# Where three small products stand in a feed-forward stage, and one more behind each layer norm's first sums

## The chip, the cores and the metric

The kernel runs on one core of one Trainium2 chip. The metric is the device time of one execution in microseconds (us); less is better. The kernel before took 3452.98 us in the median of three runs (3448.43 to 3456.45 us).

## The reference

Two blocks follow each other, each with two layers, on 256 tokens of width 2048. The first is an attention block, the second alternates mixers with feed-forward stages; the change lies in the second:

```
for layer in range(DEPTH):                                   # DEPTH = 2
    x = layer_norm(ALPHA * x + mixers[layer](x), *ln1[layer])
    x = layer_norm(ALPHA * x + conv_ffn(x, *ffns[layer]), *ln2[layer])

def layer_norm(x, g, b, eps=LN_EPS):                         # over the 2048 features of a token
    mu = xf.mean(-1, keepdims=True)
    var = jnp.square(xf - mu).mean(-1, keepdims=True)
    return ((xf - mu) * lax.rsqrt(var + eps) * g + b).astype(x.dtype)

def conv_ffn(x, w_gate, w_val, conv_w, conv_b, w_down):      # 2048 -> 5632 -> 2048
    h = causal_dwconv(x @ w_gate, conv_w) + conv_b
    return (jax.nn.silu(h) * (x @ w_val)) @ w_down
```

## The kernel before

**Layout.** Activations lie with features on the 128 partitions and the 256 tokens along the free axis: `x` is 16 tiles of 128x256. A weight matrix is cut into tiles of 128 output features, and each is fetched from memory in halves of 512 KB (1024 input features x 128). SyncE issues these fetches in a fixed order into four raw buffers; ScalarE rounds each to a high part (line 2638) and VectorE forms the low part (line 2963) in one of five buffers named `pairs`.

**A column tile.** A product in full precision is three TensorE products per 128 input features: high weights with high activations (line 2153), high with low (line 2154), low with high (line 2155). All are 128x128 weights against 128x256 columns. A half tile is 8 such triples, 24 matmuls, so a whole tile of the gate or value matrix is 48. Eight PSUM banks hold the sums; a bank holds a gate tile and the value tile of the same number side by side.

**A feed-forward stage** (`ffn`, twice in the program, layer 0 and 1) has 44 gate and 44 value tiles. Tiles 0 to 2 run ahead of the layer norm on unnormed activations ("lead") and are corrected afterwards by VectorE (line 3064 is the last step of such a correction); tiles 3 to 5 are run together while the normed parts arrive; from tile 6 on each gate tile is followed by its value tile. VectorE and ScalarE do convolution, silu and the product with the value tile (lines 3401 to 3411), and split the result into parts. Then the down projection, called the down sweep here, makes 16 output tiles from 44 input tiles each, whose activations are named `parts`; VectorE adds them to `x` in pairs of tiles (line 3091).

**The small products.** `settle` multiplies a 64x64 corner of the identity with itself into a 64x64 corner of a bank that is otherwise unused. `col_settled` is the first half of one gate tile (8 triples) with three such products between its matmuls: after the first product of the third triple, after the second of the fifth, and after the third of the seventh. It stands in gate tile number 9 (`if t == 9`, the tenth). A second free bank is taken for the results, which nobody reads.

**Each layer norm** adds up its sums as output tiles of `x` get ready. `ln_first` is its first step on TensorE: two products of a matrix of ones with `x` tiles 0 and 1 (lines 2220 and 2221; in plain 32-bit floats, so each runs as two passes), in a bank `bk0` of which columns 0 to 255 are used. VectorE reads them (`ln_s0`). There are four layer norms: behind the second halves of the two mixers' output projections (activations named `yr`), and behind the first pair of output tiles of the two down sweeps.

**Order of work.** The program is written out once by a recording layer: a plan of steps, in which side jobs are interleaved at fixed points (`pump`). Each engine runs its own list in order, and waits for semaphores of the others. So nothing is decided at run time but the waits.

Of the kernel before, what the change touches and what calls it, by code (L numbers as in the profile page):

```python
# [29 lines left out]
T = 256  # L30
# [300 lines left out]
def v3(ap, n):  # L331
    return ap.rearrange("p (a b) -> p a b", a=n)


def _build(nc, a, out, stages, ctx):
# [12 lines left out]
    def done_of(name, step=1):  # L348
        d = Done(ctx.enter_context(nc.semaphore(name)), step)
        tallies.append(d)  # L350
        return d
# [12 lines left out]
    pe, vec, act, pool = (done_of(n) for n in ("pe_done", "vec_done", "act_done", "pool_done"))  # L364
# [6 lines left out]
    def C(name, lo=0, hi=None):  # L371
        o, k = CON[name]
        return con[:, o + lo:o + (k if hi is None else hi)]
# [28 lines left out]
    x = v3(xs[:, :], KT)  # L402
# [10 lines left out]
    def do(name, *args):  # L413
        plan.append((name, args))
# [8 lines left out]
    def take(cols, side=0):  # L423
        o = mark[side]
        mark[side] += cols
        assert mark[side] <= arena[side].shape[1], mark
        return arena[side][:, o:o + cols]
# [64 lines left out]
    def load(*key):  # L492

        n = at_["mm"]
        assert stream[n] == key, (stream[n], key)
        at_["mm"] += 1
        while at_["hi"] < min(n + AHEAD, len(stream)):
            do("hi", at_["hi"])
            at_["hi"] += 1
            if at_["lo"] < at_["hi"] - 1:  # L500
                do("lo", at_["lo"])
                at_["lo"] += 1
        while at_["lo"] <= n:
            do("lo", at_["lo"])
            at_["lo"] += 1
        return n
# [30 lines left out]
    def pump(n=1):  # L537
        for _ in range(n):
            for g in list(side):
                if next(g, "end") == "end":  # L540
                    side.remove(g)
# [16 lines left out]
    def buf(pool_):  # L558
        while not pool_.free:
            yield  # L560
        return pool_.get()
# [9 lines left out]
    def col_tile(o, keys, rhs, ready, bk, step=8):  # L571

        k = 0
        for key in keys:
            n = load(*key)
            c = widths[n] // 128
            when = [ready_at(ready, k + q) for q in range(c)]
            for q in range(0, c, step):
                do("col", n, o, rhs, k, key is keys[0], key is keys[-1], when, bk.after, range(q, min(q + step, c)))
                pump()  # L580
            k += c
        return (used, n)
# [26 lines left out]
    def four(tiles_, rhs, ready, norm=None):  # L609
        bks, out = halves()  # L610
        return bks, col_group(out, tiles_, rhs, ready, norm)
# [14 lines left out]
    def lead(tiles_, norm, places):  # L626


        j = Job()
        j.id, j.norm, j.places, j.done = next(ids), norm, places, []  # L630
        j.bks = bks = [mbank() for _ in tiles_]
        norm.bk = mbank()
        kept = sorted({i for i, _ in places})
        left = list(range(len(bks)))

        def fixes():
            for i in range(len(bks) + 1):
                while len(j.done) <= min(i, len(bks) - 1) or norm.there[6 if i < 3 else 14] is None:
                    yield
                if i not in (1, 2):  # L640
                    yield
                if i == 0:
                    low_parts()
                do("lead_fix", j, i)
                if i:
                    left.pop(0)
                    if i - 1 not in kept:
                        banks.put(bks[i - 1], (vec, "lead", j.id, i - 1))

        def fixed(k):  # L650

            last_ = max(i for i, (at, _) in enumerate(places) if at == k)
            return bks[k], (vec, "lead", j.id, last_), lambda: not left or left[0] > last_

        side.append(norm.tail())
        side.append(fixes())
        col_group(lambda i: (bks[i].view[:, 0:XW], True, bks[i].after), tiles_, XG, norm.raw_at, norm, j.done)
        return [fixed(k) for k in kept]

    def both(name, *idx):  # L660
        return [(name, *idx, 0), (name, *idx, 1)]
# [15 lines left out]
    def split_job(hi, lo, src, *after):  # L677
        s = Job()
        s.id, s.hi, s.lo, s.src, s.after = next(ids), hi, lo, src, list(after)
        s.there = [(vec, "lo", s.id)]  # L680
        return s
# [335 lines left out]
    def parts_in(ap, n):  # L1017
        lo = ap.shape[1] - n * T
        return v3(ap[:, 0:n * T], n), v3(ap[:, lo:], n)
# [673 lines left out]
    def ffn(l, last):  # L1693
        u = parts_in(upart, FF)
        ut = [None] * FF
        buf5 = v3(take(5 * T), 5)
        hb = Slots([Buf(buf5[:, i, :]) for i in range(2)])
        tb = Slots([Buf(buf5[:, i, :]) for i in range(2, 4)])
        tiles_ = [(w + str(l), t) for t in range(6) for w in ("gate", "val")]
        opened = lead(tiles_[:6], last, [(2 * (i // 2), i % 2) for i in range(6)])  # L1700

        def act_tile(t, bk, m, given=None):
            while given and not given():
                yield
            j = Job()
            j.id, j.l, j.t, j.bk, j.m = next(ids), l, t, bk, m
            j.b = yield from buf(hb)
            do("ffn_conv", j)
            yield
            j.g = yield from buf(tb)  # L1710
            do("ffn_silu", j)
            hb.put(j.b, (act, "silu", j.id))
            yield
            do("ffn_gate", j)
            banks.put(bk, (vec, "ffn_u", j.id))
            yield
            s = split_job(u[0][:, t, :], u[1][:, t, :], j.g.view, (vec, "ffn_u", j.id))
            do("part_hi", s)
            yield
            do("part_lo", s)  # L1720
            ut[t] = s.there
            tb.put(j.g, *ut[t])

        for t in range(FF):
            if t == 3:
                bks, m = four(tiles_[6:], X2, last.at)
                opened += [(bk, m) for bk in bks]
            if t < len(opened):
                side.append(act_tile(t, *opened[t]))
                continue  # L1730
            else:
                while len(banks.free) < 2:
                    pump()
                bk = banks.get()
                p2 = v3(bk.view, 2)
                if t == 9:
                    spare = banks.get()
                    n = load(f"gate{l}", t, 0)
                    do("col_settled", n, p2[:, 0, :], X2, [last.at(q) for q in range(8)], bk.after, spare)
                    banks.put(spare, (used, n))  # L1740
                    pump()
                    n = load(f"gate{l}", t, 1)
                    do("col", n, p2[:, 0, :], X2, 8, False, True, [last.at(8 + q) for q in range(8)], bk.after, range(8))
                    pump()
                else:
                    col_tile(p2[:, 0, :], both(f"gate{l}", t), X2, last.at, bk)
                m = col_tile(p2[:, 1, :], both(f"val{l}", t), X2, last.at, bk)
            side.append(act_tile(t, bk, m))
        done = []

        def u_at(k):
            while ut[k] is None:
                pump()
            if k == FF - 1 and not done:
                done.extend(ev for p in ut for ev in p)
            return ut[k]

        x_free = [(used, at_["mm"] - 1)]
        norm = Norm("ln", f"ln2_g{l}", f"ln2_b{l}", nrows, [], x_free if more else None)
        out_proj(lambda t: [(f"down{l}", t, part) for part in range(6)], u, u_at, ALPHA, norm, None, last.xt)  # L1760
        return norm
# [378 lines left out]
    def tensor_program(e):  # L2140
        w = Waits(e)
        mm = partial(e.matmul, skip_group_check=True)
        ident, ones = C("ident"), C("ones")
# [73 lines left out]
        def ln_first(N):  # L2217
            w.on(N.bk0.after)
            w.on([N.x_there[0]])
            mm(N.bk0.view[:, 0:T], ones, x[:, 0, :], start=True, stop=False)  # L2220
            mm(N.bk0.view[:, 0:T], ones, x[:, 1, :], start=False, stop=True).then_inc(*pe("s0", N.id))

        def norm_sums(N):
            ps = N.bk.view
# [1645 lines left out]
```

## Time and profile before

| | us |
|---|---|
| median of three runs | 3452.98 |
| lowest, highest run | 3448.43, 3456.45 |
| the profiled execution, device time | 3450.81 |
| its span, first to last instruction | 3449.0 |
| TensorE matmul busy in the span | 3362.5 (97%) |
| VectorE busy | 2252.8 (65%) |
| ScalarE busy | 1617.1 (47%) |

The span is what the profile shows; 1.8 us lie around it. A matmul's recorded time runs on while the next one has begun (276 ns each, with starts some 113 ns apart), so an engine that is busy all the time may still run at one pace or another. The granted TensorE clock was 0.988 over the span.

Where the stages around the change lie in the trace: second half of the first mixer's output projection from 1429 us, its layer norm's first sums at 1440.6 us; feed-forward stage 0 from 1476 us, tile 6 at 1547.6 us, tile 9 at 1581.5 us, down sweep of stage 0 to 2202 us with its first sums at 1999 us; feed-forward stage 1 from 2698 us, tile 6 at 2770 us, its small products at 2803 us, down sweep to the end with first sums at 3220 us.

### The profile page before, as it was taken

Reading aid. Unit: us, or ns where it says so; the run is one execution under the profiler, and the core shown is the slowest. Engines: PE = TensorE matmul, PEld = TensorE weight load, DVE = VectorE, ACT = ScalarE, POOL = GpSimd, SP = SyncE. Lnnn points to the kernel's source line nnn. Section 1 sums busy time; section 2 is a strip of 40 time slices with the busy share of each in tenths; the row PEclk is TensorE's granted clock in tenths of the full one; section 3 lists DMA queues with packets and bytes.
Section 4 is the critical chain, followed back from the end, with each engine's and each line's share of the span. In section 5 each row is a group of like instructions: output and inputs, shape, how many; then the busy total and the mean of one; then the engine's idle time right before and its main releaser. Section 6 shows DMA issues by size and latency. Waiting matters only on the chain.

```text
span 3449.0 us, 67134 instructions
## 1 busy us (share of the span) xinstructions
PE 3362.5 (97%) x29270; PEld 3274.1 (95%) x29270; DVE 2252.8 (65%) x3653; ACT 1617.1 (47%) x2325; POOL 58.5 (2%) x78
## 2 busy tenths in 40 slices
PE   8999999999999899999999999999999999999997
PEld 8899999999999889999999999998998999999997
DVE  5656655556677777796666655686656976666455
ACT  5444444444455534364444444564443644444443
POOL 0000000000000000000000000001000000000000
PEclk9999999999999999999999999999999999999998
DMA  6555555555564322356555566543444565555663
GB/s 236 172 179 177 175 184 174 190 177 172 175 196 147 99 87 93 109 180 195 195 191 193 193 190 191 188 154 106 151 137 135 165 204 195 193 193 190 191 201 127
DMA packets 162487, 586.27 MB, mean 170 GB/s; under 512 B 18128, under 2 KB 18128, under 8 KB 161936
## 3 DMA queue, kind: packets, MB, share of 16 engines
q1 hardware_dynamic: 160560, 574.01, 51.3%
q0 software_dynamic: 1632, 7.96, 0.7%
q8 instruction: 229, 3.75, 0.4%
q14 instruction: 66, 0.54, 0.0%
HBM read 579.80 MB, written 2.10 MB: 169 GB/s over the span
## 4 chain that ended last, share of the span: by engine, by line
PE 54%; DVE 7%; ACT 1%; issue 0%; POOL 0%; ACTq 0%; DVEq 0%; POOLq 0%
PE bank L2153 16%; PE bank L2154 16%; PE bank L2155 16%; DVE pairs L2963 2%; PE bank L2372 1%; PE bank L2385 1%; DVE xs L3079 1%; DVE xs L3077 1%; PE bank L2168 0%; PE bank L2169 0%; PE bank L2170 0%; DVE xr L2967 0%; DVE right L3427 0%; ACT pairs L2638 0%; ACT xs L2689 0%
## 5 line engine op out<-in xcount | busy, mean ns | idle before, releaser
L2153 PE MATMUL bank<-xr,pairs 128*128 128x256 f32 (+1 forms) x5888 | 1661.9, 282 | 29.1 <-DVE pairs L2963 23.6
L2154 PE MATMUL bank<-xr,pairs 128*128 128x256 f32 (+1 forms) x5888 | 1639.5, 278 | 0.0
L2155 PE MATMUL bank<-xr,pairs 128*128 128x256 f32 (+1 forms) x5888 | 1639.4, 278 | 0.0
L2638 ACT ACTIVATE pairs<-raw 128x1024 fp32r<-128x1024 f32 x1106 | 1143.3, 1043 | 974.4 <-PE bank L2155 768.6
L2963 DVE TENSOR_TENSOR pairs<-raw,pairs 128x1024 fp32r<-128x1024 f32 x1106 | 1307.2, 1200 | 358.4 <-ACT pairs L2638 352.7
L2153 PEld LDWEIGHTS bank<-xr,pairs 128*128 128x128 f32 x5888 | 1114.3, 189 | 42.1 <-DVE pairs L2963 26.2
L2154 PEld LDWEIGHTS bank<-xr,pairs 128*128 128x128 f32 x5888 | 1113.8, 189 | 1.7
L2155 PEld LDWEIGHTS bank<-xr,pairs 128*128 128x128 f32 x5888 | 1114.4, 189 | 0.0
L2153 PE MATMUL bank<-parts,pairs 128*128 128x256 f32 x1792 | 496.4, 277 | 0.4 <-DVE parts L2967 0.4
L2155 PE MATMUL bank<-parts,pairs 128*128 128x256 f32 x1792 | 495.1, 276 | 0.0
L2154 PE MATMUL bank<-parts,pairs 128*128 128x256 f32 x1792 | 495.1, 276 | 0.0
L2153 PEld LDWEIGHTS bank<-parts,pairs 128*128 128x128 f32 x1792 | 336.6, 188 | 0.7 <-DVE parts L2967 0.6
L2154 PEld LDWEIGHTS bank<-parts,pairs 128*128 128x128 f32 x1792 | 336.6, 188 | 0.1
L2155 PEld LDWEIGHTS bank<-parts,pairs 128*128 128x128 f32 x1792 | 336.4, 188 | 0.0
L3401 DVE TENSOR_SCALAR arena<-bank,vec 128x256 f32<-128x256 f32 x88 | 47.8, 543 | 203.1 <-PE bank L2155 203.0
L3091 DVE SCALAR_TENSOR_TENSOR xs<-xs,bank 128x512 f32<-128x512 f32 x64 | 43.5, 685 | 154.8 <-PE bank L2155 154.7
L2663 ACT ACTIVATE nbuf<-xs 128x512 f32<-128x512 f32 x56 | 35.4, 631 | 120.8 <-DVE xs L2993 89.1
L2205 PE MATMUL bank<-pairs,xr 128*128 128x512 f32 x192 | 78.6, 409 | 0.0
L3098 DVE SCALAR_TENSOR_TENSOR arena<-bank,arena 128x256 f32<-128x256 f32 x32 | 13.6, 424 | 97.5 <-PE bank L2155 97.4
L2153 PE MATMUL bank<-yr,pairs 128*128 128x256 f32 x256 | 72.9, 285 | 4.1 <-DVE yr L2967 4.1
L2207 PE MATMUL bank<-pairs,xr 128*128 128x512 f32 x192 | 75.5, 393 | 0.0
L2206 PE MATMUL bank<-pairs,xr 128*128 128x512 f32 x192 | 75.0, 391 | 0.0
(608 smaller groups left out, 3142.4 us busy)
## 6 DMA issues: line engine op xcount, KB each, us to landing
raw<-in_w_in SPq DMA_DIRECT2D x176, 512.0 KB, 4.8
raw<-in_gate SPq DMA_DIRECT2D x176, 512.0 KB, 5.7
raw<-in_val SPq DMA_DIRECT2D x176, 512.0 KB, 4.3
raw<-in_down SPq DMA_DIRECT2D x160, 512.0 KB, 4.3
raw<-in_l_w_in SPq DMA_DIRECT2D x144, 512.0 KB, 3.9
raw<-in_w_out SPq DMA_DIRECT2D x64, 512.0 KB, 4.8
raw<-in_l_w_out SPq DMA_DIRECT2D x64, 512.0 KB, 3.7
raw<-in_v_in SPq DMA_DIRECT2D x48, 512.0 KB, 3.9
```

Of the source, the lines that this page charges most:

```text
L2153: mm(o, wh[:, q, :], rh[:, k, :], start=begin and q == 0, stop=False)
L2154: mm(o, wh[:, q, :], rl[:, k, :], start=False, stop=False)
L2155: last = mm(o, wl[:, q, :], rh[:, k, :], start=False, stop=end and q == c - 1)
L2205: mm(o, lh[:, k, ms], wh[:, q, :], start=k == 0, stop=False)
L2206: mm(o, ll[:, k, ms], wh[:, q, :], start=False, stop=False)
L2207: last = mm(o, lh[:, k, ms], wl[:, q, :], start=False, stop=k == KT - 1)
L2372: last = mm(p4[b, g, :], j.XT[b, g, 64:128], j.X[b, g, :], start=True, stop=True)
L2638: e.activation(pair_of(n)[0], v3(raw_of(n), widths[n] // slices[n]), ACT.Copy).then_inc(*hi_made(n))
L2663: e.activation(N.sq, x[:, t:t + 2, :], ACT.Square).then_inc(*act("norm_sq", N.id, t))
L2963: e.tensor_tensor(lo_, v3(raw_of(n), widths[n] // slices[n]), hi_.bitcast(F32), SUB).then_inc(*lo_made(n))
L3091: e.scalar_tensor_tensor(out=x[:, t:t + 2, :], in0=x[:, t:t + 2, :], scalar=alpha, in1=v3(bk.view, 2), op0=MUL, op1=ADD).then_inc(*vec("x_ ...
L3401: e.tensor_scalar(b, p2[:, 0, :], VC(f"cw2_{l}", t), VC(f"cb_{l}", t), MUL, ADD).then_inc(*vec("conv2", j.id))
```

## The change

In each feed-forward stage the half tile with three small products is that of gate tile 6 in place of gate tile 9. And `ln_first`, four times in the program, gets one more 64x64 product behind its two sums, into columns 256 to 319 and partitions 64 to 127 of the same bank; the semaphore that tells VectorE that the sums are there is now raised by this product.

```diff
-                if t == 9:
+                if t == 6:
                     spare = banks.get()
                     n = load(f"gate{l}", t, 0)
                     do("col_settled", n, p2[:, 0, :], X2, [last.at(q) for q in range(8)], bk.after, spare)
...
             mm(N.bk0.view[:, 0:T], ones, x[:, 0, :], start=True, stop=False)
-            mm(N.bk0.view[:, 0:T], ones, x[:, 1, :], start=False, stop=True).then_inc(*pe("s0", N.id))
+            mm(N.bk0.view[:, 0:T], ones, x[:, 1, :], start=False, stop=True)
+            hp = slice(64, 128)
+            mm(N.bk0.view[hp, T:T + 64], ident[hp, hp], ident[hp, hp], start=True, stop=True).then_inc(*pe("s0", N.id))
```

TensorE's list at the start of gate tile 6 in feed-forward stage 0, before and then after (numbered banks; `xr` holds the activations' parts, `con` the identity):

```order
L2155 MATMUL bank5<-xr,pairs 128x256
L2153 MATMUL bank0<-xr,pairs 128x256 [waits lo_made]
L2154 MATMUL bank0<-xr,pairs 128x256
L2155 MATMUL bank0<-xr,pairs 128x256
L2153 MATMUL bank0<-xr,pairs 128x256
L2154 MATMUL bank0<-xr,pairs 128x256
```

```order
L2155 MATMUL bank5<-xr,pairs 128x256
L2184 MATMUL bank0<-xr,pairs 128x256 [waits lo_made]
L2187 MATMUL bank0<-xr,pairs 128x256
L2190 MATMUL bank0<-xr,pairs 128x256
L2184 MATMUL bank0<-xr,pairs 128x256
L2187 MATMUL bank0<-xr,pairs 128x256
L2190 MATMUL bank0<-xr,pairs 128x256
L2184 MATMUL bank0<-xr,pairs 128x256
L2176 MATMUL bank6<-con 64x64 [waits vec_done]
L2187 MATMUL bank0<-xr,pairs 128x256
L2190 MATMUL bank0<-xr,pairs 128x256
```

The first small product now stands 7 matmuls into tile 6 and waits for VectorE to have let go of bank 6; before it stood 7 matmuls into tile 9, 288 matmuls later. The lists of VectorE, ScalarE, GpSimd and SyncE keep every instruction in its place; only numbers of banks differ.

TensorE's list at the layer norm's first sums in the down sweep of stage 0, before and then after:

```order
L2155 MATMUL bank0<-parts2,pairs 128x256
L2220 MATMUL bank6<-xs,con 128x256 [waits vec_done]
L2221 MATMUL bank6<-xs,con 128x256
L2153 MATMUL bank0<-parts2,pairs 128x256 [waits lo_made]
L2154 MATMUL bank0<-parts2,pairs 128x256
```

```order
L2155 MATMUL bank5<-parts2,pairs 128x256
L2220 MATMUL bank0<-xs,con 128x256 [waits vec_done]
L2221 MATMUL bank0<-xs,con 128x256
L2223 MATMUL bank0<-con 64x64
L2153 MATMUL bank5<-parts2,pairs 128x256 [waits lo_made]
L2154 MATMUL bank5<-parts2,pairs 128x256
```

One product of the small form stands between the sums and the next triple; the other three layer norms show the same.

## Rows read from the trace of the kernel before

**Rows 1.** The page: the chain that ended last, share of the span by engine
```profile
PE 54%; DVE 7%; ACT 1%; issue 0%; POOL 0%; ACTq 0%; DVEq 0%; POOLq 0%
```

**Rows 2.** TensorE by stretch: length, busy (matmuls), granted clock, DMA share, GB/s
```profile
1442.00:1475.00 33.00, 33.00 (x282) 1.00 0.51 166
1550.00:1580.00 30.00, 30.00 (x257) 1.00 0.65 205
1590.00:1960.00 370.00, 370.00 (x3267) 1.00 0.59 194
2002.00:2197.00 195.00, 195.00 (x1723) 1.00 0.63 196
2667.00:2696.00 29.00, 29.00 (x258) 1.00 0.49 162
2753.00:2800.00 47.00, 47.00 (x417) 1.00 0.68 216
2810.00:3180.00 370.00, 370.00 (x3267) 1.00 0.59 193
3224.00:3420.00 196.00, 196.00 (x1732) 1.00 0.59 184
```

**Rows 3.** TensorE, start and us: the first small product in tile 9, stage 0
```profile
1582.20 0.28 PE L2184 MATMUL bank<-xr,pairs 128*128 128x256 f32 x1
1582.41 0.33 PE L2176 MATMUL bank<-con 64*64 64x64 f32 x2
1582.67 0.38 PE L2187 MATMUL bank<-xr,pairs 128*128 128x256 f32 x1
1582.89 0.28 PE L2190 MATMUL bank<-xr,pairs 128*128 128x256 f32 x1
1583.01 0.28 PE L2184 MATMUL bank<-xr,pairs 128*128 128x256 f32 x1
```

**Rows 4.** TensorE, the first sums in the down sweep of stage 0
```profile
1999.56 0.59 PE L2221 MATMUL bank<-xs,con 128*128 128x256 f32 x2
1999.80 0.47 PE L2153 MATMUL bank<-parts,pairs 128*128 128x256 f32 x1
```

**Rows 5.** TensorE, restart after its last wait before tile 6, stage 0
```profile
1527.68 0.39 PE L2153 MATMUL bank<-xr,pairs 128*128 128x256 f32 x1 [0.99 <-DVE pairs L2963]
```

**Rows 6.** Groups by line, 1550 to 1580 us, then 1590 to 1640: count | busy, mean ns
```profile
L2154 PE MATMUL bank<-xr,pairs 128*128 128x256 f32 x86 | 24.2, 281 | 0.0
...
L2154 PE MATMUL bank<-xr,pairs 128*128 128x256 f32 x148 | 40.8, 276 | 0.0
```

**Rows 7.** The same view, 2371.7 to 2372.1 us, then 2374.2 to 2376.1
```profile
L2154 PE MATMUL bank<-xr,pairs 128*128 128x256 f32 x2 | 0.6, 281 | 0.0
...
L2154 PE MATMUL bank<-xr,pairs 128*128 128x256 f32 x7 | 1.9, 276 | 0.0
```

**Rows 8.** The same view, 2491.9 to 2493.2 us, then 2495 to 2496.9
```profile
L2154 PE MATMUL bank<-xr,pairs 128*128 128x256 f32 x4 | 1.1, 276 | 0.0
...
L2154 PE MATMUL bank<-xr,pairs 128*128 128x256 f32 x7 | 2.0, 281 | 0.0
```

**Rows 9.** TensorE, 64x64 products of the second mixer between those stretches
```profile
2372.33 0.68 PE L2385 MATMUL bank<-right 64*64 64x64 f32 x16
...
2493.58 0.69 PE L2372 MATMUL bank<-right 64*64 64x64 f32 x16
```

**Rows 10.** VectorE: lead fix, then low part of tile 6 in stages 0 and 1
```profile
1532.74 0.42 DVE L3064 TENSOR_TENSOR bank<-bank,nbuf 128x256 f32<-128x256 f32 x1
...
1542.78 2.35 DVE L2963 TENSOR_TENSOR pairs<-raw,pairs 128x1024 fp32r<-128x1024 f32 x2
...
2774.29 1.22 DVE L2963 TENSOR_TENSOR pairs<-raw,pairs 128x1024 fp32r<-128x1024 f32 x1
```

**Rows 11.** TensorE: first matmul that waits for these low parts
```profile
1547.58 0.28 PE L2153 MATMUL bank<-xr,pairs 128*128 128x256 f32 x1
...
2778.20 0.28 PE L2153 MATMUL bank<-xr,pairs 128*128 128x256 f32 x1
```

## The prediction, made before the changed kernel had run

> **What bounds the kernel now.** I read the page first. The chain that ended last is TensorE for more than half of its length and VectorE for 7%, ScalarE for 1% [rows 1]; with TensorE busy for 97% of the span (the table above), whatever the change does must be read from how fast TensorE goes, and from what makes it wait. The change removes and adds only TensorE instructions, so I next asked for TensorE's time by stretch. There all eight stretches are 100% busy at a granted clock of 1.00, and still they hold different numbers of matmuls per microsecond [rows 2]. A stretch counts every matmul that touches it, so one matmul takes (length + 0.28) / count, 0.28 us being a matmul's recorded time. This gives two paces and nothing between them: 30.28 / 257 = 117.8 ns from 1550 to 1580 us and 33.28 / 282 = 118.0 ns from 1442 to 1475, but 370.28 / 3267 = 113.3 ns from 1590 to 1960, and again 113.3 to 113.5 ns in the five others. The grouped rows show the same difference as a mean of 281 ns against 276 ns for one matmul, which makes a quick marker [rows 6]. The slow pace costs 4.5 ns a matmul, 4%. It isn't the clock, which is granted in full in both, nor the shape, which is the same, nor a wait, as there is no idle time.
>
> What separates them is an event. Stage 0 of the feed-forward runs slow up to the tile with the three small products and fast behind it, for 617 us, through the down sweep. So the small products act on the pace, and the question of the change is where that pays and where it can hurt.
>
> **Part one: the three products go from tile 9 to tile 6.** Their number stays the same, six in the program, so their own price is unchanged. In stage 0 the 288 matmuls of tiles 6, 7 and 8 lie in the slow stretch. If the products turn the pace as they do now, 288 x 4.5 ns = 1.3 us go. In stage 1 the stretch from 2753 to 2800 us is fast already [rows 2]; the products meet the fast pace there and leave it fast (2810 to 3180). Gain there: nothing.
>
> Does the new place bring a wait? The first small product waits for VectorE to release its bank. In stage 0 that is bank 6, last used by the lead's correction at 1532.74 + 0.42 us [rows 10], some 15 us before tile 6 begins at 1547.58 [rows 11]. Second, the weights: VectorE ends the low part of tile 6 at 1544.0 us, the first of the two in the row taking half of 2.35 us, and TensorE begins on it 3.6 us later; in stage 1 the tightest half tile near there ends at 2775.51 and is begun at 2778.20 us, 2.7 us of room [rows 10, 11]. The moved products take time before those half tiles, which makes the room larger, and the faster pace of a half tile takes away 24 x 4.5 ns = 0.1 us at most each, 0.3 us over the first three. No wait. VectorE's and ScalarE's lists are unchanged.
>
> **Part two: four products behind the sums.** What one costs is read at tile 9: from the start of the matmul ahead of a small product to that of the second behind it are 1582.89 - 1582.20 = 0.69 us, where two matmuls of the slow pace take 0.24. So a small product costs 0.45 us of TensorE time [rows 3], though it computes only 64x64 numbers. The gap of 0.21 us ahead and the 0.22 us after the restart hold most of it. Behind the sums [rows 4] the trace has no such product, so I bound it. From below: the sums' passes are longer than a matmul, and their end could cover the gap ahead, which leaves 0.2 us. From above: both sides pay twice, 0.9 us. I take 0.45, the nearest row. Four times on the path that is 1.8 us (0.8 to 3.6). VectorE gets its signal for the sums about 0.4 us later; it uses them only for a running sum that has tiles of work behind it, so I cost that at nothing; without that cover it would be 4 x 0.4 us = 1.6 us.
>
> The Trainium skill, page "TensorEngine Tiling", section "Key Properties", says that changing the tiling mode drains TensorE. It speaks against these four: a drain each way, at places where three of four already run fast. The rows agree, with the 0.21 us ahead of the small product and 0.22 us behind it, and I have used them for the price.
>
> What do the four do to the pace? At the first mixer the stretch behind the sums is slow, up to 1475 us. Those 34 us hold 34 / 0.1178 = 288 matmuls, and turning them saves 1.3 us. Does one product suffice? At tile 9 the first of three, met at the slow pace, left it slow: the third matmul behind it starts 0.12 us after the second, as before [rows 3]. Only the second or third turned it. Two runs of 64x64 products in the mixers are nearer in one respect, that the stream restarts behind them at the first product of a triple, as behind the sums: at 2372 us such a run turned slow into fast [rows 7, 9], while at 2493 us one turned fast into slow [rows 8, 9]. I take it that the first mixer's stretch is turned, at little more than even odds. In the second mixer and the two down sweeps the pace is fast, and the six products of the two stages never left a fast pace slow; I take it that it stays fast.
>
> **The sum.** +1.8 us (four products) - 1.3 (tiles 6 to 8 of stage 0) - 1.3 (first mixer) = -0.8 us. Against the profiled execution that is 3450.81 - 0.8 = 3450.0 us. That execution lies 2.2 us under the median of the runs shown, so against the median I expect 3452.98 - 0.8 = 3452.2 us. Comparing two versions of this kernel, less than about 0.2% (6.9 us) can't be told from no change: the three runs alone spread over 8 us.
>
> **Rival 1, other small outcomes of the same sign of nothing.** The first mixer stays slow: +0.5 us, 3453.5. Or the slow stretch in stage 0 isn't there in most executions, since it begins where TensorE restarts after a wait for VectorE at 1527.68 us [rows 5], and another restart might be a fast one; then its gain is gone too: +1.8 us, 3454.8. For it: in stage 1, behind the same steps, the pace was fast at 2753 us [rows 2].
>
> The same +1.8 us would come out if the pace didn't depend on what came before at all; the trace speaks against this with its two sharp levels. The Trainium skill, page "TensorE: Matmul & The Clock Gate", section "Back-to-back issue gap", gives an isolated gap of the columns divided by 2.4 GHz plus 2.5 ns, an estimate of 109 ns for 256 columns whatever the history. Both paces of the rows lie above it, and the slow one isn't in it.
>
> **Rival 2, slower: a new product leaves a down sweep slow.** Behind the first sums of each down sweep the pace is fast in the trace [rows 2], and each sweep has about 200 us left: 203 us / 0.1133 = 1790 matmuls in stage 0 and about 1800 in stage 1, with nothing behind them that would turn the pace back before the end of the sweep. At 4.5 ns each that is +8.1 us for one sweep, with the other terms 3452.2 + 8.1 = 3460.3 us; for both, as they are the same instructions at the same phase, 3468.4. For it: 64x64 products at 2493 us did this [rows 8, 9], and a single product, not three, stands here. Against it: the products of tile 9 in stage 1 met the fast pace at all three places of a triple and kept it. It decides as soon as one sweep shows 281 ns.
>
> **Rival 3, slower: the three at tile 6 don't turn stage 0, or a later wait undoes it.** Nothing repairs it until the end of the down sweep, 617 us of 113.3 ns = 5450 matmuls at 4.5 ns = 24.5 us; 3452.2 + 24.5 = 3476.7 us (the 1.3 us of tiles 6 to 8 is lost as well). The room of 3.6 us and more speaks against a wait, and the same three products in the same order against the first.
>
> **Rival 4, faster.** The median of the runs before holds a down sweep or another long stretch at the slow pace, which the profiled execution doesn't, and the new products turn it: 3452.2 - 8 = 3444 us. The 8 us between the lowest and the highest run are just one sweep. Against it: the profiled execution, all fast, is in the middle of the runs and not the lowest.
>
> **How the numbers follow.** Forecast 0.38, rival 1 0.29: together 0.67 within 0.2%. Rival 2 0.15 and rival 3 0.04: 0.19 slower. Rival 4 0.14 faster. The range takes in one slow sweep at 3460.3 with 2.7 us for the spread of runs and the dearer bound of the four products, and leaves out both sweeps and rival 3: 3463. Below it reaches to rival 4: 3444. The forecast's own range is 3448 to 3457.
>
> **What would show it.** In the changed profile: tiles 6 to 8 of stage 0 at a mean of 276 ns, where 281 stands now; the stretch behind the first mixer's sums at 276 (281 would take 1.3 us back); each L2223 product with about 0.45 us from the matmul ahead; no idle time of TensorE ahead of the small product at tile 6; the down sweeps at 276. The prediction is wrong if any stretch of over 150 us is at the other pace than now, whichever way, or if TensorE waits at tile 6.

## The result, and the profile of the changed kernel

The changed kernel takes 3467.32 us (median of 5 runs, 3461.97 to 3470.06) against 3452.98 for the kernel before (5 runs, 3448.43 to 3456.45). The ratio is 1.0043 with a 95% interval of 1.0033 to 1.0054: slower by 14.3 us, where I had forecast 0.8 us faster and ended the range at 3463. It is rival 2 with both sweeps slow, whose price had been worked out as 3468.4 us. I had given that rival, one sweep or two, a chance of 0.15.

The profiled execution took 3468.2 us (3450.81 before). The page's rows of busy time and of the chain that ended last, which answer to [rows 1]:

```profile
PE 3375.7 (97%) x29278; PEld 3285.3 (95%) x29278; DVE 2253.6 (65%) x3653; ACT 1616.6 (47%) x2325; POOL 59.4 (2%) x78
...
PE 87%; DVE 10%; ACT 2%; issue 1%; DMA 0%; POOL 0%; ACTq 0%; SPq 0%; DVEq 0%; POOLq 0%
```

The shares of the chain can't be compared: before, they add up to 62% of the span, so the chain was followed through that much only. The busy time can. TensorE is busy for 13.2 us more than before (3375.7 against 3362.5) with eight instructions more; VectorE and ScalarE do what they did. So most of the loss is not a wait: TensorE does the same matmuls more slowly. As to where, the same eight stretches show that answer to [rows 2] (length, busy and matmuls, granted clock, DMA share, GB/s):

```profile
1442.00:1475.00 33.00, 32.76 (x283) 1.00 0.49 164
1550.00:1580.00 30.00, 30.00 (x261) 1.00 0.66 218
1590.00:1960.00 370.00, 370.00 (x3268) 1.00 0.59 194
2002.00:2197.00 195.00, 195.00 (x1657) 1.00 0.61 188
2667.00:2696.00 29.00, 28.76 (x247) 1.00 0.48 147
2753.00:2800.00 47.00, 45.43 (x380) 0.96 0.62 198
2810.00:3180.00 370.00, 370.00 (x3268) 1.00 0.59 194
3224.00:3420.00 196.00, 196.00 (x1663) 1.00 0.60 186
```

Read them by (length + 0.28) / count, as in the prediction. The two stretches of gate and value tiles, from 1590 and from 2810 us, stand at 113.3 ns a matmul, as before. The two down sweeps have gone from 113.3 to 195.28 / 1657 = 117.9 and 196.28 / 1663 = 118.0 ns. The other four can't be read by that rule, as they hold other things now. The first has the first mixer's wait, sums and added product in it, and the second the three small products. The fifth, at 2667 us, holds the end of the second mixer's slow pace (that mixer came to its sums fast before, and slow here), a short wait, the sums and the added product; behind them the pace is fast. The sixth, at 2753 us, holds a wait of 1.8 us for VectorE and 3.4 us at half the clock behind it, both of which the kernel before has ahead of 2753. The grouped rows say the same with the quick marker, first for 1446 to 1475 us, behind the first mixer's sums, then for 2002.2 to 2197 us in the down sweep (count, busy us, mean ns, idle before):

```profile
L2154 PE MATMUL bank<-yr,pairs 128*128 128x256 f32 x86 | 23.7, 276 | 0.0
...
L2154 PE MATMUL bank<-parts,pairs 128*128 128x256 f32 x552 | 155.1, 281 | 0.0
```

Now the place where the pace turns, in TensorE's rows (start, us) at the first sums in the down sweep of stage 0, which answer to [rows 4]:

```profile
2000.23 0.28 PE L2153 MATMUL bank<-parts,pairs 128*128 128x256 f32 x1
2000.34 0.28 PE L2154 MATMUL bank<-parts,pairs 128*128 128x256 f32 x1
2000.46 0.28 PE L2155 MATMUL bank<-parts,pairs 128*128 128x256 f32 x1
2000.58 0.60 PE L2220 MATMUL bank<-xs,con 128*128 128x256 f32 x2
2001.01 0.59 PE L2221 MATMUL bank<-xs,con 128*128 128x256 f32 x2
2001.54 0.32 PE L2223 MATMUL bank<-con 64*64 64x64 f32 x2
2001.79 0.38 PE L2153 MATMUL bank<-parts,pairs 128*128 128x256 f32 x1
2002.01 0.28 PE L2154 MATMUL bank<-parts,pairs 128*128 128x256 f32 x1
2002.13 0.28 PE L2155 MATMUL bank<-parts,pairs 128*128 128x256 f32 x1
2002.25 0.28 PE L2153 MATMUL bank<-parts,pairs 128*128 128x256 f32 x1
```

Ahead of the sums the starts are 0.11 apart, behind the small product 0.12, and they stay there for the 1800 matmuls that are left of the sweep. From the start of L2221 to that of the second matmul behind it there are 1.00 us; the kernel before took 0.55 there, from 1999.56 us [rows 4] to the second of these rows, so the small product costs 0.45 us, as forecast.

```profile
1999.13 0.60 PE L2220 MATMUL bank<-xs,con 128*128 128x256 f32 x2
...
2000.11 0.28 PE L2154 MATMUL bank<-parts,pairs 128*128 128x256 f32 x1
```

The most direct measure of the loss is to lay the two traces side by side, instruction by instruction. At the first sums of stage 0 the changed kernel is 1.45 us behind (2000.58 against 1999.13), at the end of that down sweep, at 2204 us of the kernel before, 9.9; at the first sums of stage 1 8.0, at 3420 us 16.2. Each sweep costs 8.2 to 8.4 us, its small product of 0.45 us included, and all else together under 1 us.

With a record of each of the 24,000 or so matmuls of this kind, the loss can be counted: I took a record of 275 to 277 ns for fast and of 280 to 283 for slow, and charged 4.5 ns to each slow one.

| where | slow before | slow after | difference, us |
|---|---|---|---|
| gate and value tiles and down sweep, stage 0 (1600 to 2210 us) | 2 | 1766 | +7.9 |
| the same, stage 1 (from 2760 us) | 5 | 1801 | +8.1 |
| first mixer's end and start of stage 0 (1420 to 1600 us) | 854 | 101 | -3.4 |
| all else | 3344 | 3080 | -1.2 |

Together +11.4 us. With four products of 0.45 us (+1.8) and 4.2 us more of TensorE's idle time (90.7 against 86.5 us of the spans) that is 17.4 us, and the profiled executions are 17.4 us apart. That it closes so well is in part luck: the account leaves out the stretches at half the granted clock, one of which, around 2350 us, lasted 13.7 us before and 3.4 us now, while others are new. The idle time comes as several small waits for VectorE and ScalarE, most of the growth between 2250 and 2600 us, in the second mixer. That a TensorE which is faster in one stretch reaches them sooner is likely, and not shown.

### The profile page after: what moved, and what is told of

It is laid out like the page before. It is cut to its first block, busy times and chain, and to the rows that moved or that the text cites. A ratio compares the mean times of both kernels' runs of the same rounds, so it can differ in the third digit from the quotient of the medians.

```text
span 3466.4 us, 67150 instructions
## 1 busy us (share of the span) xinstructions
PE 3375.7 (97%) x29278; PEld 3285.3 (95%) x29278; DVE 2253.6 (65%) x3653; ACT 1616.6 (47%) x2325; POOL 59.4 (2%) x78
## 4 chain that ended last, share of the span: by engine, by line
PE 87%; DVE 10%; ACT 2%; issue 1%; DMA 0%; POOL 0%; ACTq 0%; SPq 0%; DVEq 0%; POOLq 0%
PE bank L2153 24%; PE bank L2154 24%; PE bank L2155 24%; DVE pairs L2965 3%; PE bank L2207 2%; PE bank L2205 2%; PE bank L2206 2%; PE bank L2374 1%; PE bank L2387 1%; PE bank L2254 1%; DVE xs L3081 1%; ACT pairs L2640 1%; PE bank L2270 1%; DVE xs L3079 1%; PE bank L2263 0%
## 5 line engine op out<-in xcount | busy, mean ns | idle before, releaser
L2153 PE MATMUL bank<-parts,pairs 128*128 128x256 f32 x1792 | 502.3, 280 | 0.4 <-DVE parts L2969 0.4
L2155 PE MATMUL bank<-parts,pairs 128*128 128x256 f32 x1792 | 501.2, 280 | 0.0
L2154 PE MATMUL bank<-parts,pairs 128*128 128x256 f32 x1792 | 501.1, 280 | 0.0
```

What stands on the lines that cost most here:

```text
L2153: mm(o, wh[:, q, :], rh[:, k, :], start=begin and q == 0, stop=False)
L2154: mm(o, wh[:, q, :], rl[:, k, :], start=False, stop=False)
L2155: last = mm(o, wl[:, q, :], rh[:, k, :], start=False, stop=end and q == c - 1)
```

## The experiments

The theory was: a small product behind the sums turns a fast pace slow, and nothing in a down sweep turns it back, so each sweep loses 8 us. The time of before that stands beside each kernel was taken with it, on the same chip.

### The move alone, the four products alone, the mixers' two

`move` takes only the first hunk of the change. `ln4` takes only the second, with `if t == 9`. `mixers` has the move, and the product only behind the two mixers' sums:

```diff
-            hp = slice(64, 128)
-            mm(N.bk0.view[hp, T:T + 64], ident[hp, hp], ident[hp, hp], start=True, stop=True).then_inc(*pe("s0", N.id))
+            if N.g.startswith("ln1"):
+                hp = slice(64, 128)
+                last = mm(N.bk0.view[hp, T:T + 64], ident[hp, hp], ident[hp, hp], start=True, stop=True)
+            last.then_inc(*pe("s0", N.id))
```

> Only the move: the three small products stand in tile 6, and nothing is added behind the sums. Every theory of the added products leaves both down sweeps fast here (276 ns a matmul, 113.3 ns from start to start), as they were before. Time: 0 to -1.3 us against the kernel before (-1.3 where tiles 6 to 8 of stage 0 are slow in the execution before). A rival that blames the move for the 15 us would show +10 us or more.

> Only the four added products; the three stand in tile 9 as before. My theory: these alone turn both down sweeps slow, +8.1 us each, +1.8 us for themselves, less 1.3 us or 2.6 us behind the mixers: +14 to +17 us against before, the same time as the changed kernel within 2 us. Rival (the move has a part in it): under +10 us.

> The move, and the added product only behind the two mixers' sums, not in the down sweeps. Both down sweeps fast. Theory 'turns over' (the product turns whatever pace stands before it into the other): behind a mixer that runs slow ahead of the sums the stretch gets fast, -1.3 us + 0.45 us each; one that runs fast gets slow, +1.3 + 0.45 us. Theory 'place' (it is always fast there and always slow in the down sweeps): fast behind both. Time against before: -3 to +1 us by both; 10 us or more under the changed kernel.

Measured: `move` 3450.36 us, ratio 0.9994 (0.9985 to 1.0003); `ln4` 3471.38, 1.0050 (1.0037 to 1.0063); `mixers` 3449.90, 0.9999 (0.9989 to 1.0008); before 3451.56. `ln4` is slower by 17 us by the ratio (20 by the medians), at or over the upper end of the 14 to 17 expected. The loss is in the second hunk, and there in the two products of the down sweeps. Windows of the two down sweeps, behind the sums, in `move`:

```profile
2010.00:2197.00 187.00, 187.00 (x1653) 1.00 0.62 196
3236.00:3420.00 184.00, 184.00 (x1626) 1.00 0.57 181
```

and the same in `ln4`:

```profile
2010.00:2197.00 187.00, 187.00 (x1590) 1.00 0.60 188
3236.00:3420.00 184.00, 184.00 (x1565) 1.00 0.59 186
```

187.28 us hold 1653 matmuls at 113.3 ns or 1590 at 117.8. The move costs nothing, and in `mixers`, where the stream comes to tile 6 of stage 0 at the slow pace, the three products turned it there, as they do at tile 9 before.

### One sweep at a time

`sweep0` has the move, and the product only behind the sums of the down sweep in stage 0 (the edit against `mixers`):

```diff
-            if N.g.startswith("ln1"):
+            if N.g == "ln2_g0":
```

> The move, and the added product in one place alone: behind the first sums of the down sweep of stage 0. Theory (a small product directly behind sums that TensorE did not wait for leaves a fast stream slow): that sweep at 281 ns, the other at 276; 1790 matmuls x 4.5 ns = 8.1 us and 0.45 us for itself: +8 us against the kernel with the move alone, about +7 against before. The rival that the 15 us come from somewhere else than the pace of the sweeps gives less than 5.

Measured: 3457.80 us against 3451.19, ratio 1.0016 (1.0008 to 1.0025).

```profile
2010.00:2197.00 187.00, 187.00 (x1590) 1.00 0.59 186
3236.00:3420.00 184.00, 184.00 (x1626) 1.00 0.60 189
```

One sweep is slow, the other not: the product in stage 0 makes its own sweep slow and leaves the other alone, and one slow sweep is about half of the loss (the interval holds 3 to 9 us). The product in stage 1 alone was not run.

### The product ahead of the sums

`ahead` is the changed kernel with the small product ahead of the two sums instead of behind them:

```diff
             w.on([N.x_there[0]])
+            hp = slice(64, 128)
+            mm(N.bk0.view[hp, T:T + 64], ident[hp, hp], ident[hp, hp], start=True, stop=True)
             mm(N.bk0.view[:, 0:T], ones, x[:, 0, :], start=True, stop=False)
...
-            mm(N.bk0.view[hp, T:T + 64], ident[hp, hp], ident[hp, hp], start=True, stop=True).then_inc(*pe("s0", N.id))
```

> The move, and the four added products ahead of the sums instead of behind them. A small product alone kept a fast pace 12 times of 12 and sums alone kept it too, so if it is the order 'sums, then small product' that does it, both sweeps stay fast: +1 to +2 us against before, for the products themselves. If any small product beside the sums does it, both sweeps are slow: +14 to +17 us.

Measured: 3468.26 us against 3451.19, ratio 1.0051 (1.0038 to 1.0063), both sweeps slow:

```profile
2010.00:2197.00 187.00, 187.00 (x1590) 1.00 0.60 187
3236.00:3420.00 184.00, 184.00 (x1565) 1.00 0.60 186
```

A theory fell here: that the product does harm only because it is the last thing ahead of the restart. The second mixer's stretch, entered fast, was left slow here too, and the first mixer's, entered slow, was left fast.

### A product over the whole array

`full` puts a product of the same 64 columns on all 128 rows and columns of the array in the place of each of the four:

```diff
-            hp = slice(64, 128)
-            mm(N.bk0.view[hp, T:T + 64], ident[hp, hp], ident[hp, hp], start=True, stop=True).then_inc(*pe("s0", N.id))
+            mm(N.bk0.view[:, T:T + 64], ident, ident[:, 0:64], start=True, stop=True).then_inc(*pe("s0", N.id))
```

> The move, and four added products that use the whole array (128x128 identity against 64 columns) in place of the 64x64 corner, at the same place behind the sums. If the trouble needs the corner form (a drain ahead of it and a restart behind), both sweeps stay fast, as one probe of this form from the fast pace did: -1 to +1.5 us against before. If any short product behind the sums does it: +14 to +17 us.

Measured: 3451.64 us against 3451.19, ratio 0.9999 (0.9990 to 1.0008), both sweeps fast. The windows, and the rows at the sums of stage 0:

```profile
2010.00:2197.00 187.00, 187.00 (x1652) 1.00 0.62 196
3236.00:3420.00 184.00, 184.00 (x1626) 1.00 0.59 187
```

```profile
2003.05 0.59 PE L2221 MATMUL bank<-xs,con 128*128 128x256 f32 x2
2003.48 0.33 PE L2222 MATMUL bank<-con 128*128 128x64 f32 x2
2003.62 0.37 PE L2153 MATMUL bank<-parts,pairs 128*128 128x256 f32 x1
2003.82 0.28 PE L2154 MATMUL bank<-parts,pairs 128*128 128x256 f32 x1
```

This product starts 0.43 us behind the first sum pass of L2221, where the 64x64 product needed 0.53, and the stream is back 0.14 us later in place of 0.25. From the start of L2221 to that of the second matmul behind it there are 0.77 us in place of 0.55, so it costs about 0.2 us, and it does no harm here. So one more instruction behind the sums isn't the cause by itself; its form counts, or the time that it takes.

### Two kernels full of small interruptions

`probe1` and `probe2` are the kernel before with an interruption in every second gate tile from tile 12 on, behind the fifth of eight triples, and in the down sweeps ahead of a pair of tiles: the two sums with constants for data (`s`), one 64x64 product (`c`), one over the whole array (`f`), and rows of these. They do extra work whose results nothing uses. In `probe1` some stand behind the first or second product of the fifth triple in place of the third; in some gate tiles of `probe2` the half tile with three small products stands instead, to bring the pace back to fast. The core of the edit:

```diff
+            for what in kind:
+                if what == "s":
+                    mm(ps[:, 0:T], ones, con[:, 0:T], start=True, stop=False)
+                    mm(ps[:, 0:T], ones, con[:, 0:T], start=False, stop=True)
+                elif what == "c":
+                    mm(ps[hp, T:T + 64], ident[hp, hp], ident[hp, hp], start=True, stop=True)
+                elif what == "f":
+                    mm(ps[:, T:T + 64], ident, ident[:, 0:64], start=True, stop=True)
```

> The kernel before, with probes of TensorE in the fifth triple of single half tiles, ten microseconds apart, results unread; pace (113 or 118 ns from start to start, 276 or 281 ns a record) read ahead of and behind each. Stage 0: sums alone; sums and a small product x3; a small product alone x3; sums; two small products x2; sums and small product; small product then sums x2; sums and a full-array product of 64 columns x2; all behind the third product of the triple. Stage 1: a small product alone behind the first (x3), second (x3) and third (x3) product of the triple, then sums and small product behind the first (x2) and second (x2), full-array product x2. Down sweeps, between tiles: sums and small product x3, small product x2, sums. Theory 'turns over': sums and a small product alternate fast, slow, fast, slow everywhere. Theory 'place': in the down sweeps always slow, in the gate tiles always the same. Theory 'wait' (slow if TensorE doesn't wait ahead of the sums, fast if it does): always slow, as nothing waits here. Sums alone change nothing by all.

> The kernel before with further probes. Gate tiles, from the fast pace each time (the three products of a settling half tile stand between): small product then sums (x3); sums and two small products; sums and three; sums and full-array product (x2, and x2 from slow); one sum and small product; three small products from slow; sums and a small product with 128 columns; sums, full-array, small product; sums and, one triple later, a small product (x2). Theory 'adjacent': only a small product directly behind sums turns fast to slow; apart, or the other way round, the pace stays fast. Theory 'any': all of them do. Down sweeps: a wait of TensorE for VectorE ahead of sums and small product (x3), ahead of a small product alone, and without a wait (x2). Theory 'wait': behind a wait the pace gets fast (as in all six cases behind the mixers), without it slow; theory 'no matter': slow both ways.

One run each, with a profile: 3510.05 and 3526.47 us; the times themselves say little, the pace behind each interruption is the measurement. Windows of 18 us of `probe1`, behind the sums alone, the sums and one 64x64 product, one 64x64 product alone, and the sums and one product over the whole array, all four entered at the fast pace:

```profile
1784.00:1802.00 18.00, 18.00 (x161) 1.00 0.64 213
1645.00:1663.00 18.00, 18.00 (x155) 1.00 0.60 198
2896.00:2914.00 18.00, 18.00 (x161) 1.00 0.65 210
1946.00:1964.00 18.00, 18.00 (x161) 1.00 0.62 202
```

161 is the fast pace, 155 the slow one. All of them, sorted by what stood there and how it was entered (the sums of the down sweeps themselves are in the first row):

| interruption | entered fast: left fast | entered slow: left fast |
|---|---|---|
| sums alone | 5 of 5 | 1 of 2 |
| one 64x64 product alone | 10 of 10 | 3 of 6 |
| two 64x64 products alone | 2 of 2 | |
| three 64x64 products alone | | 0 of 1 |
| sums, one 64x64 product | 0 of 12 | 5 of 11 |
| sums, two or three 64x64 products | 0 of 2 | |
| sums, 64x64 product one triple later | 0 of 1 | 0 of 1 |
| 64x64 product, then sums | 2 of 2 | 0 of 3 |
| half of the sums, then a 64x64 product | 1 of 1 | |
| sums, then a 64x64 product with 128 columns | 1 of 1 | |
| sums, whole-array product | 3 of 3 | 3 of 3 |
| sums, whole-array product, 64x64 product | 1 of 1 | |
| whole-array product alone | | 0 of 2 |
| wait for VectorE, sums, 64x64 product | 5 of 6 | |
| wait for VectorE, 64x64 product | 0 of 2 | |

Three theories fell with it. It isn't the place alone: with the product behind the sums the gate tiles do as the down sweeps. (With the 64x64 product ahead of the sums they don't: fast here in two gate tiles, slow in both sweeps of `ahead`; why, no run tells.) It isn't the kind of instruction alone: where TensorE comes without a wait, sums and 64x64 products each leave the fast pace alone by themselves, and together turn it slow 12 times of 12. And it isn't a switch that turns over each time: of eleven entered slow, six stayed slow. Those eleven tell one thing more. The five that went fast were entered by a stream whose last matmul and first sum pass started 120 ns apart, in the six others it was 118 or 119: the slow pace has more than one form, and from one of them the same interruption leads out. The single 64x64 products of all twelve traces, those of the half tiles included, say so more sharply. Entered fast they left the pace fast 87 times of 87. Entered slow they left it fast 21 times of 21 where they started 211 ns behind the last matmul, and 2 times of 22 where they started 209 or 210 ns behind it.

In the last two rows TensorE waits for VectorE to change a bank that TensorE has just filled, some 1.07 us from start to start. Such a bank needs a first product of ones, so these rows hold one more pass pair ahead of the wait than those without a wait, and no run has that pass pair without the wait: that it is the wait which changes the outcome is likely, and not shown. Windows of `probe2`: wait, sums, 64x64 product (5 of 6 so), wait and 64x64 product, and the sixth of the first kind:

```profile
2047.00:2065.00 18.00, 18.00 (x161) 1.00 0.69 213
2112.00:2130.00 18.00, 18.00 (x155) 1.00 0.73 218
2176.00:2194.00 18.00, 18.00 (x155) 1.00 0.67 198
```

The mixers' own sums stand behind a wait in every kernel, and they are the control for the product there. Without a product behind them (`before`, `move`, `sweep0`, `spared` and the two probes) the pace was left fast 5 times of 12, and sums alone turned a fast pace slow 5 times of 9. With the 64x64 product (the changed kernel, `ln4`, `mixers` and `repair`) it was left fast 8 times of 8. Windows behind the first and the second mixer's sums in `sweep0`, both entered fast and with no product:

```profile
1450.00:1470.00 20.00, 20.00 (x179) 1.00 0.47 158
2672.00:2692.00 20.00, 20.00 (x172) 1.00 0.48 155
```

### Turning the pace back in the changed kernel

If the slow pace alone is the loss, three 64x64 products a triple or two apart, the half tile that stands at tile 6, must bring it back when they come right behind. `repair` is the changed kernel with such a half tile in each down sweep; the first of its three products stands 31 matmuls behind the product at the sums. `spared` has the same half tiles and the move, and no product behind any sums. The core of both edits:

```diff
-            for j in range(2):
-                m = col_tile(p2[:, j, :], parts(t + j), y, ready, bk)
+            spare = banks.get() if not first and t == 2 else None
+            for j in range(2):
+                m = col_tile(p2[:, j, :], parts(t + j), y, ready, bk, spare=None if j else spare)
...
+            if spare and key is keys[3]:
+                do("col_settled", n, o, rhs, when, bk.after, spare, k, False)
```

> The changed kernel, and in each down sweep three 64x64 products, a triple or two apart, in the half tile right behind the sums and their product (31 matmuls later), as at tile 6. Theory (the loss is the slow pace alone, which began behind the sums and lasts because nothing interrupts it): the three turn it back. About 1740 of the 1800 matmuls of each sweep are fast again, 2 x 1740 x 4.5 ns = 15.7 us, less 6 x 0.45 = 2.7 us for the products: 13.0 us faster than the changed kernel, about 3454, ratio to before 1.0007, TensorE from 2020 to 2197 us at 113.3 ns a matmul. Rival (something else in the sweep, as later weights or a busier memory, holds it at the slow pace): the sweep stays at 117.9 ns, the time rises by the 2.7 us to about 3470, ratio 1.0051.

> The same six products in the down sweeps, but no product behind any sums (the move to tile 6 stays). The sweeps are then fast when the three products come. Theory (products standing alone leave a fast pace fast, and cost 0.45 us each): 6 x 0.45 = 2.7 us above the kernel with the move alone, about 3454, ratio to before 1.0005, the sweeps at 113.3 ns a matmul. Rival (any small product in a down sweep makes it slow, the sums have no part in it): both sweeps at 117.9 ns, about 3470, ratio 1.005.

Measured: `repair` 3455.58 us (12 runs), ratio to before 1.0011 (1.0002 to 1.0019); `spared` 3455.28, 1.0010 (1.0001 to 1.0018); before 3452.38. The changed kernel stood at 1.0043. Windows of `repair`, between the product and the half tile, then both sweeps:

```profile
2002.50:2006.00 3.50, 3.50 (x31) 1.00 0.56 167
2010.00:2197.00 187.00, 187.00 (x1652) 1.00 0.61 194
3236.00:3420.00 184.00, 184.00 (x1626) 1.00 0.60 189
```

The few matmuls between are slow (mean 281 ns in the grouped rows; the quotient of so short a window is no measure), and from 2010 us on the sweep is at 113.3 ns. In both sweeps the first of the three products did it: it started 211 ns behind its last matmul, and from the sixth matmul behind it the records are at 276 ns. The two others met the fast pace and kept it. Six products more made the kernel about 11 us faster (1.0043 to 1.0011; the sum gave 13.0, and the intervals of the two ratios allow it). Nothing else in the sweep holds the pace down, and `spared`, which never has a slow sweep, is level with it, 0.1% above before for six products of 0.45 us.

None of these kernels beats the kernel before by more than can be measured; `move` and `mixers` are level with it.

## Why the prediction was wrong

- **The step that failed.** It is this one: "In the second mixer and the two down sweeps the pace is fast, and the six products of the two stages never left a fast pace slow; I take it that it stays fast." Those six products stand alone between matmuls of the stream, and alone such a product keeps a fast pace (10 of 10 in the probes). Behind the sums the same product turns it slow (12 of 12, and in the sweeps of the changed kernel, `ln4`, `sweep0` and `repair` 7 of 7), and 8 us a sweep follow that the sum had at nothing. The sign that the prediction had named, a stretch of over 150 us at the other pace than now, was there twice. I had carried a behaviour from one neighbourhood to another, though I had myself looked for "nearer" examples for the first mixer and found one of each kind [rows 7, 8]. By that standard the sweeps were at even odds too, and as both come from the same instructions at the same phase, "both slow" deserved more than a share of 0.15, and the range had to reach it.
- **Rival 2** was right in mechanism and in size: 8.1 us a sweep forecast; 7.9 and 8.1 counted from the records, two sweeps, 3468.4 against 3467.32 us.
- **Price of a product:** 0.45 us, right at all four places.
- **Part one, the move:** right in that nothing is lost and no wait comes. Its gain of 1.3 us in stage 0 can't be told: in the changed kernel tile 6 was reached at the fast pace, and in `move` the ratio of 0.9994 holds both a gain of 1.3 us and none.
- **Second mixer:** forecast fast and fast, but its stream came to the sums slow in this execution, and the product turned it.
- **First mixer:** turned fast, as forecast at little more than even odds. The product has a part in it: 8 of 8 behind both mixers with it, 5 of 12 without. What differs from the sweeps is the wait of TensorE just ahead of these sums; that the wait is the reason is argued. The 753 slow matmuls fewer from 1420 to 1600 us are 288 of this stretch, 288 of tiles 6 to 8 and some of the tiles ahead of these, which the changed kernel ran fast behind TensorE's waits; in `mixers` they were slow, so that part is no gain of the change. The net of the two products behind the mixers can't be measured (`mixers` against `move`).
- **Rivals 1, 3 and 4** don't explain the result. What rival 1 said of stage 0, that the slow stretch ahead of tile 6 isn't always there, is so; it is too small to be seen. Rival 4 had taken the 8 us between the runs of before for one sweep. `move` spreads over 11 us in 11 runs and its sweeps are fast in its one profile, and no kernel with fast sweeps has a median near 3444 us, so the spread speaks for nothing of the kind.
- The Trainium skill, page "TensorE: Matmul & The Clock Gate", section "Back-to-back issue gap", gives a gap from the number of columns and the clock, with no term for what came before. By it the four products would have cost their own price and no more. The two paces of this kernel, 113.3 and 117.9 ns for the same 256 columns at one granted clock of 1.00, decide against that.

What stays open is what the two paces are. The granted clock is 1.00 in both, DMA share and bytes are alike, and the shapes are the same; what the rows show is that the outcome is repeatable where TensorE comes without a wait and at the fast pace, that it depends on the form and order of what interrupts the stream, and that behind the mixers' wait the same sums and product leave the fast pace. From the slow pace the single product's outcome goes with a start that differs by 1 or 2 ns. What inside TensorE sets the pace, no run here tells.

## What to carry to other kernels

Before an instruction is put into a dense stream, compare the pace on both sides of such an instruction in the trace, in the same neighbourhood, and price what is left of the stream behind it, not the instruction: 0.45 us of work cost 8 us here, because 1800 matmuls follow and nothing interrupts them. An instruction that mends the pace in one place isn't safe in another where the pace is good already; add it only where the rows show the slow pace. If one must stand there, see whether one that uses the whole array does as well (0.2 us, and no slow sweep), or turn the pace back right behind it.

## What the runs showed of the hardware

- A stream of 128x128 by 128x256 products has two sustained paces at the same granted clock, 113.3 and 117.9 ns a matmul, and kept the slow one for 200 us and the fast one for 370 us, until something interrupted it or the stretch ended.
- The same sums and the same 64x64 product lead from fast to slow without a wait ahead (12 of 12 in the probes, 7 of 7 in the sweeps) and from fast or slow to fast behind the wait of the mixers (8 of 8, where the sums alone did so 5 times of 12).
- A single 64x64 product between matmuls kept the fast pace 87 times of 87. From the slow pace it led to the fast one where it started 211 ns behind the last matmul (21 of 21), and mostly not at 209 or 210 ns (2 of 22).
- A 64x64 product costs such a stream 0.45 us, a product of the same 64 columns over the whole array 0.2 us.
